# Attention stage of a streaming encoder layer: query tiles in pairs of a long and a short one, five key segments a step

## The reference

```python
SEQ = 2048; CHUNK = 64; Q_BLOCK = 128; A_HEADS = 4; A_HEAD_DIM = 64

def diff_attention(q, k, v, q_pos, k_pos, lam):
    s = jnp.einsum('bqhcd,bkhcd->bhcqk', q.astype(F32), k.astype(F32)) * (A_HEAD_DIM ** -0.5)
    visible = (k_pos[None, :] // CHUNK) <= (q_pos[:, None] // CHUNK)
    s = jnp.where(visible, s, -jnp.inf)
    p = jax.nn.softmax(s, axis=-1)
    w = p[:, :, 0] - lam * p[:, :, 1]
    return jnp.einsum('bhqk,bkhe->bqhe', w, v.astype(F32))

def attn_prompt(qa, ka, va, lam):
    ...
    def one(args):
        q_blk, bi = args
        q_pos = bi * Q_BLOCK + jnp.arange(Q_BLOCK)
        return diff_attention(q_blk, ka, va, q_pos, k_pos, lam)

    o = lax.map(one, (qb, jnp.arange(nqb)))
```

## Time and profile before

| | us |
|---|---|
| median of 3 runs | 3063.68 (3063.48 to 3067.08) |
| the profiled execution | 3063.2 |
| its span, first to last instruction | 3061.5 |
| mean granted TensorE clock, share of 2.4 GHz | 0.957 |
| busy in the span: PE / PEld / DVE / ACT / POOL | 2768.0 / 1752.8 / 1508.9 / 1023.0 / 428.8 |

### The profile page before, as it was taken

One profiled execution on the slowest core, in us unless ns is written; L12 is line 12 of the kernel. 1 busy time (PEld: TensorE's weight loads), 2 busy tenths in 40 slices (PEclk: granted clock), 3 DMA queues, 4 the chain that ended last, 5 costly groups with the idle time before them and its releaser, 6 DMA issues. The chain is left out here.

```text
span 3061.5 us, 40464 instructions
## 1 busy us (share of the span) xinstructions
PE 2768.0 (90%) x13121; PEld 1752.8 (57%) x13122; DVE 1508.9 (49%) x2900; ACT 1023.0 (33%) x2269; POOL 428.8 (14%) x684
## 2 busy tenths in 40 slices
PE   8999999999999857899959999599999999999960
PEld 6677767777777635677745555344444444444420
DVE  2556555655565658888734555422323232323227
ACT  2333333333333236777725564001010101010108
POOL 2111111111111102222210111101111110101000
PEclk9999999999999969999979999699999999999985
DMA  6000100010000141000052221587755557575558
GB/s 235 32 32 24 36 32 27 24 38 31 27 24 31 45 143 56 32 8 8 8 163 90 89 89 55 191 308 264 283 206 219 206 219 289 218 288 217 217 197 301
DMA packets 167714, 382.89 MB, mean 125 GB/s; under 512 B 13378, under 2 KB 30530, under 8 KB 165456
## 3 DMA queue, kind: packets, MB, share of 16 engines
q1 hardware_dynamic: 153328, 333.76, 30.3%
q0 software_dynamic: 14304, 48.08, 4.1%
HBM read 310.73 MB, written 71.08 MB: 125 GB/s over the span
## 5 line engine op out<-in xcount | busy, mean ns | idle before, releaser
L659 PE MATMUL z_psum<-w_in_sb,hT 128*128 128x512 f32 x1088 | 480.5, 592 | 0.0
L653 PE MATMUL z_psum<-hT,w_in_sb 128*128 128x128 f32 x3264 | 374.1, 276 | 0.8 <-ACT hT L326 0.8
L653 PEld LDWEIGHTS z_psum<-hT,w_in_sb 128*128 128x128 f32 x3264 | 369.9, 193 | 1.7 <-ACT hT L326 1.2
L1898 PE MATMUL gate_psum<-w_gate_sb,block_rows_T 128*128 x720 | 321.3, 600 | 13.9 <-SPq L1730 13.9
L659 PEld LDWEIGHTS z_psum<-w_in_sb,hT 128*128 128x128 f32 x1088 | 200.5, 190 | 221.0 <-issue 221.0
L1922 PE MATMUL down_psum<-w_down_sb,hidden_T 128*128 x720 | 323.7, 592 | 0.9 <-ACT hidden_T L1804 0.9
L1902 PE MATMUL up_psum<-w_up_sb,block_rows_T 128*128 x720 | 316.3, 592 | 0.0
L1607 PE MATMUL y_psum<-w_out_sb,mix_T 128*128 128x512 f32 x544 | 244.4, 603 | 0.9 <-DVE mix_T L1464 0.9
L1902 PEld LDWEIGHTS up_psum<-w_up_sb,block_rows_T 128*128 128x128 f32 x720 | 136.8, 190 | 172.2 <-issue 172.2
L844 ACT ACTIVATE probs<-score_psum,neg_max 128x512 f32<-128x512 f32 (+3 forms) x320 | 197.0, 625 | 107.4 <-DVE neg_max L894 107.3
L1898 PEld LDWEIGHTS gate_psum<-w_gate_sb,block_rows_T 128*128 128x128 f32 x720 | 135.0, 193 | 168.4 <-issue 168.4
(11 more groups left out here) (310 smaller groups left out, 3567.2 us busy)
## 6 DMA issues: line engine op xcount, KB each, us to landing
w_gate_sb<-in_w_e_gate SPq DMA_DIRECT2D x32, 2048.0 KB, 8.4
w_up_sb<-in_w_e_up SPq DMA_DIRECT2D x32, 2048.0 KB, 14.1
w_down_sb<-in_w_e_down SPq DMA_DIRECT2D x32, 2048.0 KB, 18.2
expert_rows<-scratch_moe SPq DMA_DIRECT2D x17, 1024.0 KB, 8.4
w_in_sb<-in_w_in SPq DMA_DIRECT2D x7, 2048.0 KB, 19.0
scratch_z<-z_ring SPq DMA_DIRECT2D x34, 256.0 KB, 2.0
scratch_h<-h SPq DMA_DIRECT2D x17, 512.0 KB, 2.6
x_tile<-in_x_prompt SPq DMA_DIRECT2D x16, 512.0 KB
```

What stands on the lines that cost most here:

```text
L653: mm = pe.matmul(out[:, hd * P:(hd + 1) * P], w[:, c, col:col + P], hT[:, u, c, :], start=(c == 0), stop=(c == DC - 1))
L659: mm = pe.matmul(out[:, :], hT[:, u, c, :], w[:, c, g * HW:(g + 1) * HW], start=(c == 0), stop=(c == DC - 1))
L1898: mm = pe.matmul(gps[:, :], xT[:, u, c, :], part(wg, slot, c), start=(c == 0), stop=(c == DC - 1))
```

## The change

Query tiles are taken in pairs, (8, 7), (9, 6), ... (15, 0). A step is now a pair and a head: 32 steps, each with 17 key blocks in exactly five segments, the long tile's first. The small statistics (row_max, factor, factors) are made once for a step, over a layout of [tile of the pair, map, four segments], where a segment that does not exist holds neutral values; row_max also makes the differences that factor takes the exponential of, so factor is one instruction instead of two, and the last multiplication in factors is one instead of two.

VectorE's loop now begins with seg_max(n, 0), and factors(n-1) comes behind it. TensorE and ScalarE turn, copy and weigh step n-2 where they took n-3. probs has three rows of 17 blocks for four of 16. The output buffers belong to the two tiles of a pair (long: 0, short: 1); VectorE copies the long tile out, behind factors, ScalarE the short one, behind its first copy_T. All 16 q rows stay resident, and SP issues the four small loads first, then all row loads without a wait, then the stores. The first pair needs two q rows and the k and v rows 0 to 8, each later pair two q rows and one k and one v row.

```diff
 def attend(nc, dr, consts):
 
     ident = consts["ident"]
-    NSEG = [len(seg_of(i)) for i in range(NT)]
-    STEPS = [(i, h) for i in range(NT) for h in range(HEADS)]
+    PAIRS = [(NT // 2 + j, NT // 2 - 1 - j) for j in range(NT // 2)]
+    STEPS = [(j, h) for j in range(len(PAIRS)) for h in range(HEADS)]
     N = len(STEPS)
-    SEG0 = [sum(NSEG[i] for i, _ in STEPS[:n]) for n in range(N + 1)]
-    AHEAD = 8
-    PIECE = 2
-
-    def segs(n):
-        return NSEG[STEPS[n][0]] if 0 <= n < N else 0
+    S = 5
+
+    def segs_of(j):
+
+        big, small = PAIRS[j]
+        return ([(0, s, k0, kw, k0) for s, (k0, kw) in enumerate(seg_of(big))]
+                + [(1, s, k0, kw, big + 1 + k0) for s, (k0, kw) in enumerate(seg_of(small))])
+
+    assert all(len(segs_of(j)) == S for j in range(len(PAIRS)))
+
+    def seg(n, s):
+        return segs_of(STEPS[n][0])[s]
+
+    def live(n):
+        return 0 <= n < N
...
         sem = stage_semaphores(nc, ctx)
-        q = sb("att_q", [P, AHEAD, HW])
...
-        pr = sb("probs", [P, 4, 2, SEQ])
+        pr = sb("probs", [P, 3, 2, (NT + 1) * P])
...
         ops = [ps(f"att_out_psum{s}", [P, HW]) for s in range(2)]
...
         @block.sync
         def _(sp):
-            def load(i):
-                if i >= AHEAD:
-                    sp.wait_ge(s_ps, SEG0[(i - AHEAD + 1) * HEADS])
-                sp.dma_start(q[:, i % AHEAD, :], dr["z"][QA][i]).then_inc(rows_in[i], 16)
-                sp.dma_start(k[:, i, :], dr["z"][KT][i]).then_inc(rows_in[i], 16)
-                sp.dma_start(v[:, i, :], vp[i]).then_inc(rows_in[i], 16)
-
-            load(0)
             for n, name in enumerate(("lam_q1", "lam_k1", "lam_q2", "lam_k2")):
                 sp.dma_start(lamv[:, n, :], dr[name].to_broadcast([P, 64])).then_inc(lam_in, 16)
-            for i in range(1, AHEAD):
-                load(i)
-            for i in range(NT):
-                sp.wait_ge(o_ok, i + 1)
-                sp.dma_start(dr["att"][i], o[:, i % 2, :]).then_inc(att_out[i % 2], 16)
-                if i + AHEAD < NT:
-                    load(i + AHEAD)
-            for u in range(2):
-                sp.wait_ge(att_out[u], 16 * (NT // 2))
+            for j, (big, small) in enumerate(PAIRS):
+                for i in (big, small):
+                    sp.dma_start(q[:, i, :], dr["z"][QA][i]).then_inc(rows_in[j], 16)
+                for i in range(0 if j == 0 else big, big + 1):
+                    sp.dma_start(k[:, i, :], dr["z"][KT][i]).then_inc(rows_in[j], 16)
+                for i in range(0 if j == 0 else big, big + 1):
+                    sp.dma_start(v[:, i, :], vp[i]).then_inc(rows_in[j], 16)
+            for j, pair in enumerate(PAIRS):
+                for m, i in enumerate(pair):
+                    sp.wait_ge(o_ok[m], j + 1)
+                    sp.dma_start(dr["att"][i], o[:, m, :]).then_inc(att_out[m], 16)
+            for m in range(2):
+                sp.wait_ge(att_out[m], 16 * len(PAIRS))
...
             def expo(n, s):
-                g = SEG0[n] + s
-                k0, kw = seg_of(STEPS[n][0])[s]
-                if s == 0:
-                    wait(act, tg_ps, SEG0[n - 3] if n >= 4 else 0)
+                g = S * n + s
+                m, l, k0, kw, at = seg(n, s)
+                if s == 0 and n >= 3:
+                    act.wait_ge(tg_ps, S * (n - 2))
                 act.wait_ge(m_ok, g + 1)
                 for c in range(2):
-                    ins = nc.scalar.activation(pr[:, n % 4, c, k0 * P:(k0 + kw) * P], sps[g % 2][:, c, 0:kw * P],
-                                               ACT.Exp, bias=nmax[:, n % 2, c, s:s + 1], accum_out=zsum[:, n % 2, c, s:s + 1])
+                    ins = nc.scalar.activation(pr[:, n % 3, c, at * P:(at + kw) * P], sps[g % 2][:, c, 0:kw * P],
+                                               ACT.Exp, bias=nmax[:, n % 2, m, c, l:l + 1], accum_out=zsum[:, n % 2, m, c, l:l + 1])
                 ins.then_inc(e_ok, 1)
 
             def factor(n):
                 act.wait_ge(nM_ok, n + 1)
-                for c in range(2):
-                    ins = nc.scalar.activation(fac[:, n % 2, c, 0:segs(n)], nmax[:, n % 2, c, 0:segs(n)], ACT.Exp,
-                                               scale=-1.0, bias=tot[:, n % 2, c:c + 1])
-                ins.then_inc(ef_ok, 1)
+                f = fac[:, n % 2, :, :, :].rearrange("p m c s -> p (m c s)")
+                nc.scalar.activation(f, f, ACT.Exp, scale=-1.0).then_inc(ef_ok, 1)
...
+            def out_row(j, m):
+                act.wait_ge(pv, S * HEADS * (j + 1))
+                wait(act, att_out[m], 16 * j)
+                nc.scalar.copy(o[:, m, :], ops[m][:, :]).then_inc(o_ok[m], 1)
+
             for n in range(N + 3):
-                cur, old = segs(n), segs(n - 3)
-                for s in range(max(cur + 1, old)):
-                    if s < old:
-                        copy_T(n - 3, s)
-                    if 1 <= s <= cur:
+                for s in range(S + 1):
+                    if live(n - 2) and s < S:
+                        copy_T(n - 2, s)
+                    if s == 0 and live(n - 3) and STEPS[n - 3][1] == HEADS - 1:
+                        out_row(STEPS[n - 3][0], 1)
+                    if live(n) and s >= 1:
                         expo(n, s - 1)
-                if cur:
+                if live(n):
                     factor(n)
...
             def seg_max(n, s):
-                g = SEG0[n] + s
-                kw = seg_of(STEPS[n][0])[s][1]
+                g = S * n + s
+                m, l, k0, kw, at = seg(n, s)
+                b = n % 2
                 dve.wait_ge(s_ps, g + 1)
-                if s == segs(n) - 1:
+                if l == len(seg_of(PAIRS[STEPS[n][0]][m])) - 1:
                     chain.after(nc.vector.memset(sps[g % 2][0:64, :, kw * P - 64:kw * P], HIDDEN))
-                if s == 0 and n >= 2:
-                    dve.wait_ge(ef_ok, n - 1)
-                red(nmax[:, n % 2, :, s:s + 1], sps[g % 2][:, :, 0:kw * P], AX.X, ALU.max, negate=True).then_inc(m_ok, 1)
+                red(nmax[:, b, m, :, l:l + 1], sps[g % 2][:, :, 0:kw * P], AX.X, ALU.max, negate=True).then_inc(m_ok, 1)
...
             def row_max(n):
-                dve.wait_ge(m_ok, SEG0[n + 1])
-                red(tot[:, n % 2, 0:2], nmax[:, n % 2, :, 0:segs(n)], AX.X, ALU.min).then_inc(nM_ok, 1)
+                b = n % 2
+                dve.wait_ge(m_ok, S * (n + 1))
+                if n >= 2:
+                    dve.wait_ge(w1_ok, S * (n - 1))
+                chain.after(red(tot[:, b, 0, :, :], nmax[:, b, :, :, :], AX.X, ALU.min))
+                tt(fac[:, b, :, :, :], nmax[:, b, :, :, :], tot[:, b, 0, :, :, None].to_broadcast([P, 2, 2, 4]), ALU.subtract).then_inc(nM_ok, 1)
 
             def factors(n):
-                w, b = segs(n), n % 2
+                b = n % 2
                 dve.wait_ge(ef_ok, n + 1)
-                dve.wait_ge(e_ok, SEG0[n + 1])
-                chain.after(tt(zsum[:, b, :, 0:w], zsum[:, b, :, 0:w], fac[:, b, :, 0:w], ALU.mult))
-                chain.after(red(tot[:, b, 2:4], zsum[:, b, :, 0:w], AX.X, ALU.add))
-                chain.after(nc.vector.reciprocal(tot[:, b, 4:6], tot[:, b, 2:4]))
-                chain.after(tt(tot[:, b, 2:4], tot[:, b, 4:6], coef[:, :], ALU.mult))
-                for c in range(2):
-                    ins = ts(fac[:, b, c, 0:w], fac[:, b, c, 0:w], tot[:, b, 2 + c:3 + c], None, ALU.mult)
-                ins.then_inc(fac_ok, 1)
+                dve.wait_ge(e_ok, S * (n + 1))
+                chain.after(tt(zsum[:, b, :, :, :], zsum[:, b, :, :, :], fac[:, b, :, :, :], ALU.mult))
+                chain.after(red(tot[:, b, 1, :, :], zsum[:, b, :, :, :], AX.X, ALU.add))
+                chain.after(nc.vector.reciprocal(tot[:, b, 2, :, :], tot[:, b, 1, :, :]))
+                chain.after(tt(tot[:, b, 1, :, :], tot[:, b, 2, :, :], coef[:, None, :].to_broadcast([P, 2, 2]), ALU.mult))
+                tt(fac[:, b, :, :, :], fac[:, b, :, :, :], tot[:, b, 1, :, :, None].to_broadcast([P, 2, 2, 4]), ALU.mult).then_inc(fac_ok, 1)
...
+            def out_row(j, m):
+                dve.wait_ge(pv, S * HEADS * (j + 1))
+                wait(dve, att_out[m], 16 * j)
+                nc.vector.tensor_copy(o[:, m, :], ops[m][:, :]).then_inc(o_ok[m], 1)
+
+            for n in range(N + 3):
+                if live(n) and STEPS[n] in ((4, 0), (4, 1)):
+                    clear_unused(n)
+                if live(n):
+                    seg_max(n, 0)
+                if live(n - 1):
                     factors(n - 1)
-                if cur:
-                    seg_max(n, 0)
-                for s in range(max(cur - 1, mid)):
-                    if s + 1 < cur:
+                if live(n - 3) and STEPS[n - 3][1] == HEADS - 1:
+                    out_row(STEPS[n - 3][0], 0)
+                for s in range(S):
+                    if live(n) and s + 1 < S:
                         seg_max(n, s + 1)
```

(71 more changed lines are left out.)

42 lines of the change are left out of this document (23 added, 19 removed).

## The result

The changed kernel takes 3017.97 us (median of 4 runs, 3016.05 to 3020.51) against 3064.1 in the same session: ratio 0.9847, 95% interval 0.9833 to 0.9862. Forecast were 3015 and a range of 3000 to 3038. The profiled execution took 3016.05, its span 3014.2.

The account below looks back on a forecast made before the run. TensorE was taken to set the pace; loads 19.4, fill 20.5, thirty steps 337.5, slow part 3.0, pair changes 9.8, drain 12.6 and end 5.0 sum to 407.8 us against 455.6, giving 3015 us, range 3000 to 3038.

Parts of the forecast that it names:

- The likeliest case: Whole change works as laid out, TensorE setting the pace at 11.25 us a step: 3015 us, chance 0.60.
- Loads: Stage start: four small loads and 20 rows land before the first scores, 19.4 us after the first issue (17 to 22).
- Fill: First two steps, before TensorE begins step 2, with TensorE's clock at 0.50: 20.5 us (18 to 24).
- Thirty steps: Steady steps paced by TensorE: 11.25 us each, 11.1 and 0.15 for collisions, 337.5 in all.
- the slow part of step 2: Third step, counted from 0, before TensorE's clock rises: an allowance of 3.0 us.
- the pair changes: A new pair's first weighted sum waits for the long tile's output copy: 1.4 us, seven times, 9.8 in all.
- Drain: Last two steps, transposes and weighted sums without new scores: 6.3 us each, 12.6 in all.
- end: From the end of the last weighted sum to the next stage's first instruction: 5.0 us.
- The hole: TensorE's 0.91 us wait for the exponentials in an old long step; predicted to close with the maximum ahead of the statistics.
- the rival that the hole stays: TensorE's wait reappears elsewhere in each step: 12.0 us a step, 22.5 us more, 3038 us; chance 0.15.
- The rival with GpSimd as VectorE's brake: GpSimd's multiplies slow VectorE's weighings until VectorE bounds: step 12.85 us, 48 more, 3063; chance 0.11, in part or wholly.
- The rival of the low clock: TensorE stays at 1.2 GHz: 10.95 us more a step, 3103 us with two pairs at that clock; chance 0.04.

Follow-up runs that it names:

- experiment 3: Changed kernel with the output copies exchanged, ScalarE copying the long tile and VectorE the short one: 3012.8 us, ratio 0.9826.
- experiment 6: Changed kernel with an extra VectorE memset of 128x192 into spare memory behind each weighing: 3019.0 us, ratio 0.9856.
- experiment 8: Changed kernel with the second key block of every full segment left out of the weighted sum: 3038.76 us, ratio 0.9922; attention stage 389.6 us, 18.8 less.
- Experiment 2: Changed kernel with the old order restored, the small statistics ahead of VectorE's first maximum: 3028.43 us, ratio 0.9888; attention stage 420.0 us.
- after: The changed kernel itself, with the whole change, against the kernel before: 3017.97 us, ratio 0.9847; attention stage 408.4 us.
- experiment 9: Changed kernel with exchanged output copies, later v-row wait and finer start, plus 26 unused identity products on TensorE before the first scores: 3000.36 us, ratio 0.979.
- experiment 10: Changed kernel with 60 unused identity products on TensorE before the first scores, while the first rows load: 3017.7 us, ratio 0.9847.

## Why the prediction was right

The likeliest case came true. By the sum's terms, predicted and measured:

- Loads: 19.4, measured 20.7 (first S at 1108.48). 20 rows were paced at 387 GB/s to the last, as assumed. The window from the first issue to the first S holds 284 GB/s over 20.68 us, 5.87 MB, where the 20 rows and the four small loads are 5.37. So about 0.5 MB of the rows behind them, 1.3 us at 387 GB/s, had moved before the S; the sum put these at nothing.

```profile
1087.80:1108.48 20.68, 0.00 (x0) 0.00 (x0) 1.08 (x7) 0.20 (x1) 0.00 (x0) 0.50 0.77 284
```

- Fill: 20.5, measured 20.6 (first T at 1129.07). The total is right, but the clock in it wasn't as assumed (below), so it may be right by luck.
- Thirty steps, the slow part of step 2 and the pair changes: 337.5 + 3.0 + 9.8 = 350.3, measured 349.3, to the first T of the drain at 1478.33. A step is 11.26 (predicted 11.25). A pair change costs 1.25 (1.4), for the reason given, as experiment 3 showed. Step 2 cost 1.4 extra (3.0). Where the S of pair (12,3), one block in fourth place, meet the W of pair (11,4), one block in last place, two steps took 11.74 and 11.67.
- Drain: 12.6, measured 13.4 to the last W's end at 1491.68; end: 5.0, measured 4.5. The misses of the terms have both signs and nearly cancel: 408.5 measured against 407.8.

That TensorE sets the pace is shown from both sides: work added to VectorE costs nothing (experiment 6), work taken from TensorE shortens the step, late in the stage by nearly all of it (experiment 8). VectorE's predicted 10.5 us a step was too high: it is busy for 9.79.

The hole closed, but the prediction split the credit wrongly. By its price for the rival that the hole stays, 0.75 a step and 22.5 in all, the new order would bring 22.5 of the 47.8 us and the rest 25.3. Experiment 2 shows 11.6 and 35.6: with the old order most steps are longer by only 0.3 to 0.6. In the old kernel the order alone is worth 36.1.

The rival with GpSimd as VectorE's brake fell. The mean w rose from 0.694 to 0.723, not to 1.16; over a step that is 0.15, not 2.35. (Both means mix shapes; a w of 128x512 that meets no multiply takes 0.74, so the 1.16 stood for 0.42 more, not 0.47.) GpSimd's own multiply rose from 0.636 to 0.744. The timelines of GpSimd and VectorE in one step:

```profile
1389.78 3.47 POOL L836 TENSOR_SCALAR probs<-probs,seg_factor 128x512 f32<-128x512 f32 x5 [7.79 <-DVE seg_factor L930]
```

```profile
1390.74 0.94 DVE L936 SCALAR_TENSOR_TENSOR probs<-probs,seg_factor 128x512 f32<-128x512 f32 x1
...
1392.94 0.85 DVE L936 SCALAR_TENSOR_TENSOR probs<-probs,seg_factor 128x512 f32<-128x512 f32 x1
...
1395.09 0.74 DVE L936 SCALAR_TENSOR_TENSOR probs<-probs,seg_factor 128x512 f32<-128x512 f32 x1
```

The five multiplies are over after 3.47 us. Two w's meet them and pay 0.20 and 0.11, the other three come later; VectorE idles 1.47 in this step. By the rule of the Trainium skill (SBUF — State Buffer, section "SBUF: two separate sides") a w that meets a multiply would lose up to the rest of it; 0.20 and 0.11 are within that. The rival didn't bind because most w's met none.

The rival of the low clock fell too: the granted clock is 1.00 from 1132 on, in the first step that has T and W as well as S.

## What to carry to other kernels

Before merging or reshaping steps, look for the one serial sequence that each step pays and try to move a line of it: two ways of closing the same hole don't add up. A buffer dedicated to one kind of tile moves its copy onto the path, so give that copy to the engine whose queue is free at that moment. Where records overlap, price a part by what the row grows with it (0.22 for a block of W), not by its own length (0.28). Where later work depends on data, judge an edit that changes the result by its own stage.

## What the hardware did unexpectedly

The clock of TensorE didn't rise just once during the fill; it rose, fell and rose. The windows of after:

```profile
1108.00:1112.00 4.00, 3.52 (x16) 2.54 (x16) 1.23 (x1) 0.05 (x1) 0.00 (x0) 0.50 1.06 387
1112.00:1116.00 4.00, 1.68 (x14) 1.16 (x14) 1.82 (x3) 3.54 (x12) 0.00 (x0) 0.88 1.05 386
1116.00:1120.00 4.00, 2.06 (x18) 1.30 (x16) 2.96 (x5) 2.48 (x7) 0.00 (x0) 0.97 1.05 386
1120.00:1124.00 4.00, 3.28 (x15) 1.69 (x12) 3.39 (x8) 2.11 (x8) 1.30 (x2) 0.50 1.06 389
```

The level of 2.4 GHz (1.00) came right behind two segments of S back to back. Then TensorE waited 1.18, 1.14 and 1.94 us ahead of the next S's, and the clock was at 1.2 GHz (0.50) again; from 1132 on, with few waits left, it stayed at 1.00. Experiments 9 and 10 show the same with other work: 1.00 after the products, and 0.50 again in experiment 9 during the second wait behind them, of 2.93 us, in experiment 10 during the first, of 5.98 us (the window 1108 to 1112 is at 0.50).
